# The gate's output product and the bonus change places inside every head group of the recurrent core

## The reference, cut to what matters

```
    g = jax.nn.sigmoid(xg @ g1) @ g2
    ...
    def step(S, inp):
        r_t, w_t, k_t, v_t, kk_t, b_t = inp
        sa = jnp.einsum('bhvk,bhk->bhv', S, -kk_t)
        S = S * w_t[:, :, None, :] + sa[..., None] * b_t[:, :, None, :] + v_t[..., None] * k_t[:, :, None, :]
        return S, jnp.einsum('bhvk,bhk->bhv', S, r_t)
    ...
    y = ((y - mean) * lax.rsqrt(var + GN_EPS)).reshape(B, T, C) * gn_g + gn_b
    bonus = jnp.sum(rh * kh * r_k, -1, keepdims=True) * vh
    y = (y + bonus.reshape(B, T, C)).astype(x.dtype)
    return (y * g) @ w_o
```

## Time and profile before

| | |
|---|---|
| median of 3 runs | 1148.3 us (1147.48 to 1148.36) |
| profiled execution, its own time | 1146.73 us |
| its span | 1144.9 us |
| PE busy | 1125.7 us (98%) |
| DVE busy | 820.4 us (72%) |
| ACT busy | 626.5 us (55%) |
| POOL busy | 132.5 us (12%) |

### The profile page before, as it was taken

The page is one execution under the profiler, slowest core; times in us unless marked ns, Lnnn a source line. Parts: engine busy times, 40 slices in busy tenths (PEclk is TensorE's granted clock), DMA queues, the critical chain, the costliest instruction groups (busy, mean ns, idle before and its releaser), DMA issues.

```text
span 1144.9 us, 22087 instructions
## 1 busy us (share of the span) xinstructions
PE 1125.7 (98%) x9178; PEld 995.7 (87%) x9178; DVE 820.4 (72%) x1168; ACT 626.5 (55%) x927; POOL 132.5 (12%) x97
## 2 busy tenths in 40 slices
PE   8999999999999999999999999999999999999997
PEld 8798778788888899987888889999998998888886
DVE  7889886487666587898766766888587555766665
ACT  8984664454434455657543344575656655534444
POOL 0032374402300000220121000012000000000000
PEclk9999999999999999999999999999999999999999
DMA  8631111344554564334545547536534334554541
GB/s 308 230 98 55 62 57 57 109 139 186 215 217 163 206 221 165 131 134 161 192 177 220 192 160 264 192 111 221 183 112 157 141 145 154 196 202 168 218 173 47
DMA packets 29796, 187.17 MB, mean 163 GB/s; under 512 B 3472, under 2 KB 5648, under 8 KB 8592
## 3 DMA queue, kind: packets, MB, share of 16 engines
q1 hardware_dynamic: 26784, 176.42, 42.0%
q10 hardware_dynamic: 2928, 9.54, 2.4%
HBM read 184.90 MB, written 1.05 MB: 162 GB/s over the span
## 4 chain that ended last, share of the span: by engine, by line
PE 88%; DVE 7%; ACT 3%; issue 1%; DMA 0%; SPq 0%; ACTq 0%
PE ps L2297 16%; PE ps L2279 15%; PE ps L2281 15%; PE ps L2280 15%; PE ps L2298 9%; DVE w_lo L1470 1%; PE ps L2906 1%; PE ps L2736 1%; PE ps L2822 1%; PE ps L2371 1%; PE ps L2376 1%; PE ps L2372 1%; PE ps L2614 1%; PE ps L2529 1%; PE ps L2662 1%
## 5 line engine op out<-in xcount | busy, mean ns | idle before, releaser
L1470 DVE TENSOR_TENSOR w_lo<-w_raw,w_hi 128x2048 fp32r<-128x2048 f32 x147 | 340.6, 2336 | 72.5 <-ACT w_hi L643 72.5
L643 ACT CAST w_hi<-w_raw 128x2048 fp32r<-128x2048 f32 x144 | 274.2, 1906 | 96.7 <-PE ps L2281 65.0
L2297 PE MATMUL ps<-x_both,w_hi 128*128 128x512 f32 x816 | 284.9, 391 | 0.0
L2298 PE MATMUL ps<-x_both,w_lo 128*128 128x256 f32 x816 | 230.0, 282 | 0.0
L2297 PEld LDWEIGHTS ps<-x_both,w_hi 128*128 128x128 f32 x816 | 153.1, 188 | 32.7
L2298 PEld LDWEIGHTS ps<-x_both,w_lo 128*128 128x128 f32 x816 | 154.1, 189 | 1.2
L2279 PE MATMUL ps<-w_hi,hid_hi 128*128 128x512 f32 (+1 forms) x312 | 119.9, 384 | 0.0
L2280 PE MATMUL ps<-w_lo,hid_hi 128*128 128x512 f32 (+1 forms) x312 | 119.9, 384 | 0.0
L2281 PE MATMUL ps<-w_hi,hid_lo 128*128 128x512 f32 (+1 forms) x312 | 119.8, 384 | 0.0
L2279 PE MATMUL ps<-x_both,w_hi 128*128 128x256 f32 x384 | 108.0, 281 | 0.0
L2280 PE MATMUL ps<-x_both,w_hi 128*128 128x256 f32 x384 | 107.2, 279 | 0.0
(11 more groups left out here) (494 smaller groups left out, 2188.4 us busy)
## 6 DMA issues: line engine op xcount, KB each, us to landing
w_raw<-in_weights SPq DMA_DIRECT2D x163, 1024.0 KB, 5.0
xt<-in_xT SPq DMA_DIRECT2D x2, 512.0 KB, 5.6
w_raw<-in_weights SPq DMA_DIRECT2D x2, 512.0 KB, 6.4
x_tm<-in_x SPq DMA_DIRECT2D x1, 1024.0 KB, 5.0
gain<-in_mix_g ACTq DMA_DIRECT2D x2, 512.0 KB, 4.0
gain<-in_mix_b ACTq DMA_DIRECT2D x2, 512.0 KB, 5.1
gain<-in_ffn_g ACTq DMA_DIRECT2D x2, 512.0 KB, 5.4
gain<-in_ffn_b ACTq DMA_DIRECT2D x2, 512.0 KB, 8.8
```

What stands on the lines that cost most here:

```text
L643: nc.scalar.copy(slab_hi(i), w_raw[:, i % RAW, :]).then_inc(hi_done, 1)
L1470: V.tensor_tensor(slab_lo(i), w_raw[:, i % RAW, :], slab_hi(i).bitcast(F32), ALU.subtract).then_inc(lo_done, 1)
L2297: nc.tensor.matmul(ps[:, bank, :].rearrange("p (s c) -> p s c", s=2), wh, x_both[:, :, k, :], start=start, stop=False)
L2298: return nc.tensor.matmul(ps[:, bank, 0:T], wl, x_hi[:, k, :], start=False, stop=stop)
```

## The change

Two lines of tables change. In groups 0, 1 and 2 the gate's product goes from slot 9 to slot 7 and the bonus from slot 7 to slot 9. Group 3 keeps its order (its table is cut one entry later, and the entries are the same).

```diff
-        SIDE_SLOTS = [(S_BK,), (S_BA0,), (S_KA0,), (S_YT,), (S_BA1,), (), (S_KA1,), (S_BON,), (), (S_G,)]
-        LAST_SIDE_SLOTS = SIDE_SLOTS[:7] + [(S_G,), (S_BON,), ()]
+        SIDE_SLOTS = [(S_BK,), (S_BA0,), (S_KA0,), (S_YT,), (S_BA1,), (), (S_KA1,), (S_G,), (), (S_BON,)]
+        LAST_SIDE_SLOTS = SIDE_SLOTS[:8] + [(S_BON,), ()]
```

## The result

The changed kernel takes 1149.21 us as the median of 20 runs (1147.23 to 1152.34). The kernel before, run beside it until it too had 20 runs, takes 1147.02 (1146.52 to 1148.46; the three runs shown earlier, 1147.48 to 1148.36, lie in its upper half). The ratio is 1.0018 with a 95% interval of 1.0012 to 1.0024: 0.2% slower, at the edge of what was called no change.

A forecast was written before the change was run, and what follows sets the result against it. TensorE, 98% busy, was taken as the bound, except VectorE in group 0's last slots. Terms 0.55 + 0.32 = 0.87 us, on a median taken at 1148.3, gave 1149.2 us; range 1147.6 to 1150.6.

The forecast's parts named there:

- Group 0, slot 7: a gain of nothing: Bonus leaves group 0's slot 7: TensorE reaches slot 8 0.99 us earlier, but VectorE's backlog leaves no gain.
- Group 0, slot 9: 0.48 on TensorE: Bonus waits for L1608 in group 0's slot 9, value parts queue behind; group 1's turning starts 0.48 us later.
- ScalarE adds 0.07: After group 0's slot 9, ScalarE takes the turned inverse 0.55 us later, against TensorE's 0.48; 0.55 was taken.
- Groups 1 and 2, 0.16 each: Gate's 1.15 us replaces the bonus's 0.99 in slot 7, not regained in slot 9: 0.16 per group, 0.32 together.
- The sum, 0.87: Whole kernel: 0.55 us for group 0 plus 0.32 for groups 1 and 2 makes 0.87 us slower.
- Cancels: Rival: VectorE and ScalarE have room in group 1 and swallow group 0's wait; 0 to 0.32 us left; chance 0.20 either way.
- held-up slot 8: Rival: the gate's copy delays `near_scores` in groups 1 and 2, 2.3 us slower in all, 1150.6 us; chance 0.09.
- The value parts didn't pass the waiting bonus: Rival denied here: value parts pass the bonus in group 0's slot 9, leaving 0.32 us, 1148.6; shares cancelling's chance, 0.20.
- The step that failed: Work behind the changed slots is TensorE's, busy to 98%, and carries the whole 0.87 us to the end.

The follow-up runs named there:

- e4: Whole change, but in group 0's slot 9 the bonus stands behind the last value parts; median 1147.41 us, ratio 1.0013 to the kernel before.
- e7: Kernel before with group 0's bonus in empty slot 5 and a bare wait for L1608 in slot 9; median 1147.28 us, ratio 1.0006.
- e8: Kernel before with the new order in group 0 alone, bonus behind the last value parts; median 1146.51 us, ratio 0.9999.
- e9: Kernel before with the new order in group 0 alone, six matmuls of unused product filling slot 9's wait; median 1147.89 us, ratio 1.0007.
- e5: Whole change plus six matmuls of unused product ahead of the bonus in group 0's slot 9; median 1148.41 us, ratio 1.0021 to the kernel before.
- e6: Whole change plus matmuls of unused product ahead of slot 9's bonus, six in group 0, two each in groups 1 and 2; median 1147.86 us, ratio 1.0009.
- e1: Whole change timed again without any edit; median 1150.29 us, ratio 1.0029 to the kernel before.
- e2: Kernel before with the new order in group 0 alone, groups 1 and 2 as before; median 1148.74 us, ratio 1.0021.
- e10: Kernel before with the new order in groups 1 and 2 alone, two matmuls of unused product in each slot 9; median 1146.96 us, ratio 1.0001.

## Why the prediction was right, and where it wasn't

The time given, 1149.2 us, is the measured median, but it is so by two errors that cancel: the kernel before was taken at 1148.3, and over 20 runs it is at 1147.02; and the sum said 0.87 more, where the medians differ by 2.2. The first is a matter of three runs. The second is a step that was missing.

- **Group 0, slot 7: a gain of nothing.** Right. TensorE comes to slot 8 0.89 us earlier (0.99 was forecast), 6.13 after slot 6 against 7.02, and VectorE takes the scores no sooner: at 118.31, which is the 118.52 of before less the 0.21 of the earlier start.
- **Group 0, slot 9: 0.48 on TensorE.** Right to the hundredth, as was the cause (e4). The bonus stood where it was put, 119.26 - 0.21 for the earlier start = 119.05. The idle time was put at 1.1 and is 0.94; 0.10 of the difference is that slot 8 comes only 0.89 earlier.
- **ScalarE adds 0.07.** Right at the copy, gone right behind it. ScalarE takes the turned inverse at 122.39, which is 16.06 after slot 6 against 15.51 before (122.05 - 106.54): 0.55 later, as forecast. Three copies on it has made up the 0.07: L806 began at 122.91 before, so it is 16.85 after slot 6 against 16.37, 0.48 later. At group 1's slot 6 it is 0.40. That the 0.55 goes on to the end in full was wrong.

```profile
122.39 0.38 ACT L855 COPY dd_b<-ps 128x256 f32<-128x256 f32 x1
122.65 0.37 ACT L825 COPY u_m<-ps 64x256 f32<-64x256 f32 x1
...
123.18 0.59 ACT L806 COPY bk_tm<-ps 128x512 f32<-128x512 f32 x1
```

- **Groups 1 and 2, 0.16 each.** For group 1 it is shown well: from slot 6 to the turning the six profiles with the old order there have 9.23 or 9.24 us, the eight with the new one 9.39 to 9.41. The shorter bonus gave nothing back, as argued, and the waits of 0.31 and 0.17 around it show it. For group 2 the 0.11 of this one pair isn't shown: the same stretch took 9.33 to 9.97 with the old order and 9.39 to 9.72 with the new one.
- **The sum, 0.87.** 0.68 between the two profiles, of which 0.40 for group 0 instead of 0.55. "Cancels" is out for group 0 and group 1, and so is "held-up slot 8": it decided from 0.33 us of lateness, and the copy ended 0.3 ahead of the near products. The value parts didn't pass the waiting bonus either: they start at 119.97, behind its 119.05.
- **The step that failed** is the one on what lies behind: that TensorE "carries it to the end" at an unchanged speed. I read the clock nowhere, since in the one profile at hand it was full in the recurrent core. By the mean clock it fell in 19 of the 29 executions of the whole change (11 of 20 and 8 of 9), and the one profile that caught it has it behind two of the new slots 9. That is a mechanism none of the rivals had; it is worth about 1.5 us in the median and 7.7 in the worst profile.

What is shown is this. With group 0 alone changed, the drops come with the wait and the two-column product behind it together: take either away, or fill the wait, and no drop was seen in 33 executions (e7, e8, e9), against 8 in 19. In the whole change, filling the waits of 0.31 in groups 1 and 2 as well takes the drops from 6 in 11 to none (e5 against e6), and with them the median from 1.5 above the kernel before to 1.0. The Trainium skill (TensorE: Matmul & The Clock Gate, "What's actually happening") says that the hardware sets the gate by how busy the array has recently been. The traces agree, in that both falls of e1 and that of e2 follow a slot 9 with a wait and the bonus, and fillers without any use to the result prevent the drops.

What stays open: groups 1 and 2 alone had 3 drops in 22, group 0 with its bonus but without the wait none in 22 (e8, e9), and the two together 12 in 23 (e4, e5). That is more than their sum, and no profile of e4 or e5 caught a fall that would say where it is. The drops of the kernel before, 4 in 96, weren't located either. No version had fillers in another place than a wait, so that it is their place that counts, and not that there are more matmuls, rests on e7 and e8, which have none and no drops. And with no drops left, e6 and e9 are still 1.0 above the kernel before, more than the 0.68 and the 0.48 of their order.

No version beats the kernel before. e8 and e10 are level with it (0.9999 and 1.0001).

## What to carry to other kernels

A swap of two fillers isn't priced by their lengths alone: ask what each must wait for in its new place, and put work that waits for nothing ahead of it (e8: the 0.48 us were gone). Don't price a product by its columns: eight matmuls of 2 columns held TensorE almost as long as eight of 256 (0.99 against 1.15 us here). Yet behind the same wait of 0.94 us the clock dropped in 8 of 19 executions with the narrow ones and in none of 11 with wide ones, so try the wide one in the slot that has the wait. Where one profile is quick and the median isn't, look at the mean clock of every execution before explaining the median from that profile. And before a small step of one pair of traces is believed, read the same stretch in other traces of the same order: group 1's 0.17 came back in all of them, group 2's 0.11 didn't.

## What the runs showed of the hardware that was not expected

The granted clock fell to half behind a wait of no more than 0.94 us, when eight matmuls of two columns (0.92 us) followed it; once it stayed down for 3.4 us (e2) and once for 13.6 (e1). Another time in e1 it fell for 6.7 us, 3 us after the start of such a bonus that had waits of 0.30 and 0.17 around it. In the long ones TensorE was recorded as busy throughout (4.00 of 4.00 us in the rows above). Each microsecond at the lower level cost 0.38 in e1. The same kernel on the same chip had an execution with no drop and one with two falls (e1). Behind the last matmul the clock also fell in all 14 profiles, which costs nothing but shows in the mean.
